# Loading and normalising the first half of x ahead of the modulation weights in a hybrid decoder layer

## The reference

```python
cond = jax.nn.silu(c)
ada = cond @ w_ada[l] + b_ada[l]                 # 1024 -> 6 * 1024
shift1, scale1, gate1, shift2, scale2, gate2 = jnp.split(ada[:, None, :], N_MOD, axis=-1)
h = rms_norm(x) * (1.0 + scale1) + shift1
proj = h @ w_in[l]                               # attention and gated linear attention follow
...
x = x + gate1 * mix
h = rms_norm(x) * (1.0 + scale2) + shift2
x = x + gate2 * (jnp.square(jax.nn.relu(h @ w_mlp_in[l])) @ w_mlp_out[l])
return rms_norm(x) * final_norm_g
```

## Time and profile before

| quantity | value |
|---|---|
| median of three runs | 1211.66 us |
| lowest and highest run | 1210.81 and 1213.51 us |
| span of the profiled execution, first to last instruction | 1207.3 us |
| TensorE busy, share of the span | 1145.6 us, 95% |
| VectorE busy | 566.5 us, 47% |
| ScalarE busy | 376.7 us, 31% |
| mean granted TensorE clock, as a share of full speed | 0.988 |
| DMA rate in the first fortieth of the span | 359 GB/s |

### The profile page before, as it was taken

The page is one execution under the profiler, slowest core; times in us unless marked ns, Lnnn a source line. Parts: engine busy times, 40 slices in busy tenths (PEclk is TensorE's granted clock), DMA queues, the critical chain, the costliest instruction groups (busy, mean ns, idle before and its releaser), DMA issues.

```text
span 1207.3 us, 15516 instructions
## 1 busy us (share of the span) xinstructions
PE 1145.6 (95%) x6115; PEld 957.5 (79%) x6115; DVE 566.5 (47%) x887; ACT 376.7 (31%) x717; POOL 63.7 (5%) x72
## 2 busy tenths in 40 slices
PE   1799999999998999899999999999999999999995
PEld 1678868977786999688888888888888888888884
DVE  6657556687776423713332332422422423424436
ACT  1630101467666104544214113213114123023023
POOL 0002110021221000000000000000000000000001
PEclk9989999999999999799999999999999999999998
DMA  9838540100004511021212121121111211211103
GB/s 359 244 97 300 196 140 1 36 1 1 1 1 144 136 35 36 1 70 35 70 35 66 40 64 43 35 70 35 52 55 35 70 35 35 70 36 35 53 1 139
DMA packets 60746, 87.83 MB, mean 73 GB/s; under 512 B 13987, under 2 KB 43148, under 8 KB 60684
## 3 DMA queue, kind: packets, MB, share of 16 engines
q1 hardware_dynamic: 55916, 70.09, 18.3%
q0 software_dynamic: 4768, 16.82, 4.0%
HBM read 82.69 MB, written 4.21 MB: 72 GB/s over the span
## 4 chain that ended last, share of the span: by engine, by line
PE 91%; DVE 3%; ACT 2%; DMA 1%; SPq 1%; issue 0%; POOL 0%; ACTq 0%
PE bank L499 40%; PE bank L474 38%; PE bank L688 4%; PE bank L653 2%; DMA x_in<-in_x 1%; PE bank L629 1%; PE bank L618 1%; PE bank L569 1%; DVE act_lo L887 1%; PE bank L713 1%; PE bank L537 0%; SPq L302 0%; DVE act_full L885 0%; PE bank L664 0%; SPq L293 0%; DVE x L1245 0%
## 5 line engine op out<-in xcount | busy, mean ns | idle before, releaser
L474 PE MATMUL bank<-act_hi,w_hi 128*128 128x512 f32 x672 | 264.9, 394 | 0.4 <-issue 0.4
L474 PE MATMUL bank<-act_lo,w_hi 128*128 128x512 f32 x672 | 263.6, 392 | 0.0
L474 PE MATMUL bank<-act_hi,w_lo 128*128 128x512 f32 x672 | 263.3, 392 | 0.0
L1280 ACT ACTIVATE w_hi<-raw 128x2048 fp32r<-128x2048 f32 x45 | 86.2, 1915 | 464.2 <-PE bank L499 229.0
L499 PE MATMUL bank<-w_hi,hid_hi 128*128 128x512 f32 x512 | 199.2, 389 | 0.0
L499 PE MATMUL bank<-w_lo,hid_hi 128*128 128x512 f32 x512 | 199.2, 389 | 0.0
L499 PE MATMUL bank<-w_hi,hid_lo 128*128 128x512 f32 x512 | 199.2, 389 | 0.0
L1162 DVE TENSOR_TENSOR hid_lo<-bank,hid_hi 128x512 fp32r<-128x512 f32 x64 | 44.2, 690 | 238.7 <-ACT hid_hi L1470 238.7
L1190 DVE TENSOR_TENSOR x<-bank,x 128x512 f32<-128x512 f32 x120 | 81.1, 689 | 154.0 <-PE bank L499 153.5
L474 PEld LDWEIGHTS bank<-act_hi,w_hi 128*128 128x128 f32 x672 | 127.7, 190 | 27.4 <-issue 0.9
L474 PEld LDWEIGHTS bank<-act_lo,w_hi 128*128 128x128 f32 x672 | 127.5, 190 | 26.7 <-issue 0.2
(11 more groups left out here) (173 smaller groups left out, 1240.1 us busy)
## 6 DMA issues: line engine op xcount, KB each, us to landing
ada_w<-in_w_ada POOLq DMA_DIRECT2D x32, 512.0 KB, 6.8
raw<-in_w_mlp_in SPq DMA_DIRECT2D x64, 256.0 KB, 3.4
raw<-in_w_mlp_out SPq DMA_DIRECT2D x64, 256.0 KB, 3.4
raw<-in_w_in SPq DMA_DIRECT2D x36, 256.0 KB, 5.0
ada_w_first<-in_w_ada SPq DMA_DIRECT2D x8, 1024.0 KB, 10.4
x_in<-in_x SPq DMA_DIRECT2D x8, 512.0 KB, 15.5
raw<-in_w_out SPq DMA_DIRECT2D x16, 256.0 KB, 4.4
x<-in_x SPq DMA_DIRECT2D x8, 512.0 KB, 4.3
```

The costliest lines, as they stand in the source:

```text
L474: mm = pe.matmul(bank[2 * half + m][:, :], w, act(b)[:, k, half * HALF:half * HALF + HALF], start=(n == 0), stop=(n == 3 * KT - 1))
L1280: a.activation(w_hi[:, par, :], raw[:, par, :], ACT.Copy).then_inc(s_hi, 1)
```

## The change

SyncE issues tiles 0 to 3 of x before the weights of modulation part 0; tiles 4 to 7 stay behind part 1. On VectorE the variance, the root's refinement and the scaling of the first half stand between the two modulation parts, ahead of split_lo. On ScalarE the four squares and the root of the first half stand ahead of split_hi of slot 0. On TensorE the transposes of k = 0 to 3 of the first half stand ahead of the column sums of part 1; those of k = 4 to 7 stay where they were. All arithmetic is the same.

```diff
+            for t in range(4):
+                sp.dma_start(x_in[:, t, :], x_d[:, t, :]).then_inc(s_x[t], 16)
             ada_first(0)
...
             ada_first(1)
-            for t in range(NT):
+            for t in range(4, NT):
                 sp.dma_start(x_in[:, t, :], x_d[:, t, :]).then_inc(s_x[t], 16)
...
-            def turn_half(src, half, g, nrm):
+            def turn_half(src, half, g, nrm, tiles=range(KT)):
 
                 pe.wait_ge(s_nrm[half], nrm)
-                for k in range(KT):
+                for k in tiles:
...
-            def turn_and_first_slot(src, norms, halves, first, s, par):
+            def turn_and_first_slot(src, norms, halves, first, s, par, begun=0):
 
                 for half in range(2):
-                    turn_half(src, half, halves[half], norms)
+                    turn_half(src, half, halves[half], norms, range(begun if half == 0 else 0, KT))
...
+            turn_half(x_nrm, 0, G_N1_HALVES[0], 1, range(4))
             ada(1)
-            turn_and_first_slot(x_nrm, 1, G_N1_HALVES, G_F_FIRST, 0, 0)
+            turn_and_first_slot(x_nrm, 1, G_N1_HALVES, G_F_FIRST, 0, 0, begun=4)
...
             ada_part(0)
+            norm_var(0, 0)
+            norm_scale(x_in, x_nrm, 0, 0)
             split_lo(0, 0)
             v.wait_ge(s_b_full, 1)
             v.tensor_copy(b_col, bank[5][:, 0:6 * KT]).then_inc(s_b_col, 1)
             ada_part(1)
-            norm_var(0, 0)
-            norm_scale(x_in, x_nrm, 0, 0)
...
-            split_hi(0, 0, None)
...
             for t in range(4):
                 square(x_in, x_nrm, t, landed_x)
             norm_root(0, 0)
+            split_hi(0, 0, None)
```

## The result

Over 20 runs of each, the changed kernel takes 1215.79 us in the median (1211.74 to 1222.07), the kernel before 1211.62 (1209.70 to 1217.94). The ratio is 1.0036 with a 95% interval of 1.0022 to 1.0050: slower by 2.7 to 6.1 us, 4.4 at the middle. The forecast was 1217.0, that is 5.3 us. The profiled execution spans 1212.5 us, 5.2 more than the one of before.

The account below looks back on a forecast made before the run. It took TensorE's chain of products, busy 95% of the span, as the bound, its start held by DMA rate and VectorE. 3.7 + 0.45 + 1.2 = 5.3 us took the median 1211.66 to 1217.0; range 1213.3 to 1219.6.

Parts of the forecast that it names:

- slow transposes: Transposes of k = 4 to 7 on TensorE at the lower clock: last group 1.12 us instead of 0.66, +0.45 us.
- slow first products: First products on TensorE at the lower clock: between none and 2.4 us, the middle taken, +1.2 us.
- Transfers, +5.1 us: Start: four x tiles, 2.097 MB at 411 GB/s, delay every transfer behind them up to part 1 by 5.1 us.
- Squares, transposes and both old waits at no cost: Start: four squares and early transposes cost nothing; VectorE's waits of 2.37 us for w_hi and 1.81 us for squares go.
- Part 1 ends at 39.6: VectorE: modulation part 1 takes 10.5 us, from 29.1 to 39.6, bound by VectorE and not by its weights' landing.
- Column sums exposed, first affine step at 43.6: TensorE's sums of part 1, 3.6 us, lose the norm's cover; ada_col then releases ScalarE's first affine step at 43.6 us.
- First product +3.7: TensorE: first product 6.86 us after the first affine step, at 50.5 us instead of 46.78, +3.7 us.
- The second half's fall: Clock fall at 63 us in the second half, costing 2.8 us in slow products and last transposes, expected to stay.
- The rival built on it: Second half: no clock fall there and none at the first products, +0.9 us in all, 1212.6 us; chance 0.13.

Follow-up runs that it names:

- The loads alone: The kernel before with only SyncE's load list of the changed kernel, tiles 0 to 3 of x ahead of the weights: 1215.0 us against 1211.91, ratio 1.0028.
- two tiles: The kernel before with two tiles of x loaded ahead of the weights and nothing else changed: 1212.31 us, ratio 1.0002.
- split_lo behind part 1: The changed kernel with split_lo of slot 0 moved behind modulation part 1 on VectorE: 1212.70 us, ratio 1.0008 to the kernel before.
- the slot loaded behind: The kernel before with w_in slot 0 loaded behind part 1 and x tiles 0 to 3, its split and squares 6 and 7 later: 1209.26 us, ratio 0.9970.

## Why the prediction was right, step by step

The mechanism was the forecast one at every step but one, the slow transposes. The term for the slow first products was too large.

- **Transfers, +5.1 us.** The first slice came 4.86 us later. The table of stretches now gives 416 GB/s in 5 to 12.5 us instead of 411, and the first bytes move a little sooner. The loads alone showed that this term carries the loss, and two tiles that it counts only beyond the 1.8 us of the old wait.
- **Squares, transposes and both old waits at no cost.** All as said: squares done by 10.1 us, 16 transposes from 27.27 to 30.8, no wait for w_hi.
- **Part 1 ends at 39.6.** It ended at 39.1. Of the difference 0.25 us is the smaller transfer term; the rest is that the forecast added up instructions which overlap a little in the rows.
- **Column sums exposed, first affine step at 43.6.** 3.57 us and 43.12. The sign hung on this step and on the transfers together: by the measured terms, without the 3.6 us the first affine step would have been 0.4 us early, and without the 4.9 us of the transfers 1.7.
- **First product +3.7.** It was +3.2.
- **Slow transposes, +0.45.** This step failed. The last group took 1.11 us instead of 0.66, as said, but the first product followed without the 0.42 us pause that stands ahead of it in the earlier trace rows. The two cancelled, and the term was nothing.
- **Slow first products, +1.2.** Three of them ran slow. The end of the first 48 products was 3.71 us late (61.48 against 57.77), so this term was 0.5 us here. With split_lo behind part 1 and with the slot loaded behind six were slow, with the loads alone and with two tiles none. 0 to 1.2 us is what these profiles show; the middle of the bounds was too high.
- **The second half's fall.** The sum took it as a fixed part of the kernel. Of ten profiles only two have it. The rival built on it had something right, since 1.0 us did come back in the profile, but it would have needed no fall at the first products as well.
- **Two slips in the working.** VectorE's waits between its first slice and the end of the norm are 0.37, 2.37, 0.51 and 1.81 us, 5.1 in all and not 4.2; the sum uses only the single ones. And the ends of the range do not follow from the terms given: 3.7 us without clock loss is 1215.4, and the runs' scatter of 0.9 us below the median takes it to 1214.5; 7.3 us with their 1.9 above it would be 1220.8. The stated range, 1213.3 to 1219.6, holds the measured 1215.8 either way.

So the mechanism's sum is 3.2 + 0 + 0.5 = 3.7 us, against the forecast 5.3. The measured 4.4 has an interval of 2.7 to 6.1, which holds both, so the time does not say which is nearer. That the two spans differ by 5.2 us, almost the forecast, is luck: 2.5 us of it came from places that the forecast does not name. The rule of the Trainium skill on ring order (DMA: Bandwidth & Descriptors, Queues, rings and completion order) held: everything behind the tiles was late by nearly their full time. The rule of the Trainium skill that the full clock does not engage for transposes (TensorE: Matmul & The Clock Gate, Part 4: PE-mode transpose) is not borne out: in the changed kernel the clock table's first entry, full speed, begins at 30.6 us, inside the 16 transposes, and in the kernel before at 42.6 us, when TensorE had run nothing but transposes since 38.7 and had been idle for 2.46 us before. The products ahead of the transposes may have a share in that, which no run here separated.

## What to carry to other kernels

A transfer put first is paid by everything behind it while the DMA engines are full. What it gives back is at most the wait of its own user: tile 3 of x was the last thing that VectorE waited for, but only for 1.8 us, against 4.9 us of delay for the weights. So order the loads by when their use stands on the path, and put last what is wanted last: the slot of w_in had landed at 17.9 us, TensorE first used it at 46.8, and the order that moves it behind was the faster one. When work is taken from the end of an engine's list, look at what lay beside it on the other engines; here a 3.6 us reduction on TensorE was hidden by the very norm that was moved. Differences under half a per cent are not to be read off the spans of single profiles: one fall of the clock, in a place that the change doesn't touch, was worth 1.7 to 2.9 us here.

## What was not expected of the hardware

- The granted clock reads 1.00 in every stretch before the table's first event, also where durations show half speed: in the kernel before, loading a stationary operand for the column sums takes 333 ns at 17 and at 33 us, and down to 188 ns in later stages; transposes take 427 and then 287 ns. The first event of that trace, full speed, is at 42.6 us.
- The column sums, eight products of 128x1 with two records each, took 3.57 us at half clock and 1.95 us at full clock, nearly in proportion, though they stream only one column each.
- The clock's falls come at other places from execution to execution of nearly the same program: at 63 us in the kernel before, at 68, 191 and 386 us in the changed one, at 188, 256 and 389 us with the loads alone, beside one or two between 480 and 520 us in every profile. The one at 386 us fell where TensorE waited and cost nothing, the one at 191 us cost 1.7 us.
